# A hybrid decoder layer on one core: attention values with query rows on partitions

## The reference, cut to what matters

```python
sh1, sc1, g1, sh2, sc2, g2 = split(silu(c) @ ada_w + ada_b, 6)
xn = rmsnorm(x, norm1_g) * (1 + sc1) + sh1
q, k, v, ca, cg = split(xn @ w_in)            # x: 1 x 256 x 1024; q, k, v: 8 heads x 64
q, k = rmsnorm(q, q_norm_g), rmsnorm(k, k_norm_g)       # per head
s = q @ k.T * 64**-0.5 + rel_bias[head, t5_bucket(dist)]   # own block of 256: causal
y_attn = softmax(s) @ v
a = causal_dwconv(ca * sigmoid(cg), 31 taps)            # 512 channels
a = silu(group_norm(a, 8 groups))
x = x + g1 * (concat([y_attn, a]) @ w_out)
xn2 = rmsnorm(x, norm2_g) * (1 + sc2) + sh2
u, g = split(causal_dwconv(xn2 @ w_up, 3 taps))         # w_up: 1024 x 5632
x = x + g2 * ((silu(g) * u) @ w_down)                   # w_down: 2816 x 1024
```

## Time and profile before

| | us |
|---|---|
| three runs of the kernel before | 370.85, 366.93, 375.74 |
| median | 370.85 |
| the profiled execution: its time | 369.77 |
| its span in the profile | 368.0 |
| mean granted clock of TensorE in it | 0.981 of full |

### The profile page before, as it was taken

The page is one execution under the profiler, slowest core; times in us unless marked ns, Lnnn a source line. Parts: engine busy times, 40 slices in busy tenths (PEclk is TensorE's granted clock), DMA queues, the critical chain, the costliest instruction groups (busy, mean ns, idle before and its releaser), DMA issues.

```text
span 368.0 us, 6109 instructions
## 1 busy us (share of the span) xinstructions
PE 350.7 (95%) x2401; PEld 297.6 (81%) x2401; DVE 262.7 (71%) x489; ACT 177.6 (48%) x258; POOL 43.3 (12%) x74
## 2 busy tenths in 40 slices
PE   7979899999999998799999999999999999999995
PEld 6658888997553656587999989898989999999984
DVE  2664699979999475548978785857666766768565
ACT  5444733353035648165585655455364553735530
POOL 6281352250000100002300000000000000000000
PEclk9999999999999859899999999999999999999999
DMA  7999987798978750341173555364554545500003
GB/s 283 427 420 421 419 321 287 283 354 346 418 319 339 332 205 24 116 171 57 47 299 130 214 228 216 127 231 135 208 199 156 217 164 188 216 8 1 2 0 114
DMA packets 12797, 79.51 MB, mean 216 GB/s; under 512 B 1368, under 2 KB 2784, under 8 KB 3552
## 3 DMA queue, kind: packets, MB, share of 16 engines
q1 hardware_dynamic: 12560, 78.97, 56.0%
q10 hardware_dynamic: 144, 0.13, 0.1%
q0 software_dynamic: 64, 0.01, 0.0%
HBM read 78.05 MB, written 1.06 MB: 215 GB/s over the span
## 4 chain that ended last, share of the span: by engine, by line
PE 83%; DVE 9%; ACT 3%; issue 2%; DMA 1%; POOL 0%; DVEq 0%; ACTq 0%; POOLq 0%
PE bank L932 25%; PE bank L933 23%; PE bank L934 23%; PE bank L956 3%; PE bank L976 2%; DVE bank L681 1%; PE bank L987 1%; DMA xt<-in_x_t 1%; DVE w_lo L594 1%; PE bank L1199 1%; PE bank L1079 1%; DVE prob L778 1%; PE bank L1001 1%; DVE w_lo L614 1%; PE bank L1132 1%
## 5 line engine op out<-in xcount | busy, mean ns | idle before, releaser
L932 PE MATMUL bank<-act_hi,w_hi 128*128 128x256 f32 x480 | 137.4, 286 | 2.9 <-ACT act_hi L391 1.1
L933 PE MATMUL bank<-act_lo,w_hi 128*128 128x256 f32 x480 | 135.7, 283 | 0.0
L934 PE MATMUL bank<-act_hi,w_lo 128*128 128x256 f32 x480 | 135.7, 283 | 0.0
L594 DVE TENSOR_TENSOR w_lo<-raw,w_hi 128x2048 fp32r<-128x2048 f32 (+1 forms) x44 | 95.2, 2164 | 30.8 <-ACT w_hi L364 30.8
L932 PEld LDWEIGHTS bank<-act_hi,w_hi 128*128 128x128 f32 x480 | 91.8, 191 | 10.7 <-issue 5.3
L364 ACT ACTIVATE w_hi<-raw 128x2048 fp32r<-128x2048 f32 x45 | 85.9, 1908 | 15.2 <-DMA raw<-in_stream 12.4
L933 PEld LDWEIGHTS bank<-act_lo,w_hi 128*128 128x128 f32 x480 | 92.0, 192 | 0.4
L934 PEld LDWEIGHTS bank<-act_hi,w_lo 128*128 128x128 f32 x480 | 91.9, 192 | 0.0
L681 DVE SCALAR_TENSOR_TENSOR bank<-glu,cols,bank 128x256 f32<-128x256 f32 x116 | 46.5, 479 | 0.0
L553 ACT ACTIVATE bias<-bank,cols 128x256 f32<-128x256 f32 x44 | 22.2, 555 | 34.0 <-PE bank L934 34.0
L932 PE MATMUL bank<-w_hi,hid_hi 128*128 128x512 f32 x88 | 34.9, 396 | 0.0
(11 more groups left out here) (172 smaller groups left out, 393.1 us busy)
## 6 DMA issues: line engine op xcount, KB each, us to landing
raw<-in_stream SPq DMA_DIRECT2D x71, 1024.0 KB, 5.1
xt<-in_x_t SPq DMA_DIRECT2D x2, 512.0 KB, 4.6
bias<-toeplitz_rows SPq DMA_DIRECT2D x1, 1024.0 KB, 10.8
xr<-in_x_rows SPq DMA_DIRECT2D x1, 1024.0 KB, 9.8
out<-xmod SPq DMA_DIRECT2D x3, 256.0 KB, 2.0
gates_b<-in_ada_b_gates SPq DMA_DIRECT2D x1, 256.0 KB, 8.5
cols<-in_cols SPq DMA_DIRECT2D x1, 185.0 KB, 5.3
out<-xmod SPq DMA_DIRECT2D x1, 128.0 KB, 1.9
```

What stands on the lines that cost most here:

```text
L594: nc.vector.tensor_tensor(w_lo[:, m % PARTS, cut], slot(*SPLIT[m])[:, cut], w_hi[:, m % PARTS, cut].bitcast(f32), ALU.subtract).then_inc(l ...
L932: nc.tensor.matmul(o, sh, mh, start=first, stop=False)
L933: nc.tensor.matmul(o, sh, ml, start=False, stop=False)
L934: return nc.tensor.matmul(o, sl, mh, start=False, stop=last)
```

## The change

Value matmuls: the transposed probabilities (keys x query rows) become the stationary operand and v (64 columns) the moving one, so that bank 5 gets query rows on partitions and the head's 64 columns beside each other: three matmuls of 64 columns a head. The probabilities are not multiplied by the reciprocals any more; the values are, by DVE out of bank 5 into `att_rows` (scale_rows). For each pair of heads TensorE then transposes att_rows (turn_rows, two transposes) into the upper half of bank 5, where att_hi_part and att_lo_part read. Besides, the lists of the head loop are ordered anew, the modulation rows are turned behind the loop into bank 0, and POOL also subtracts the last 768 columns of "out" 0, 1 and 2.

```diff
-        POOL_LOW = range(3, 10)
+        POOL_LOW = range(3, 13)
+        att_rows = glu_gate[:, :, 0:P]
-        HIGH_AT_HEAD = {0: out 0, 3: out 1, 5: out 2}      LOW_AT_HEAD = {3: out 0, 4: out 1, 7: out 2}
+        HIGH_AT_HEAD = {0: out 0, 1: out 1, 4: out 2, 7: out 3}   LOW_AT_HEAD = {2: out 0, 3: out 1, 5: out 2}
 # POOL
+            for m in POOL_LOW:
+                if m == SP_AT["out", 0]: gn_square(0)
+                elif m == SP_AT["out", 2]: gn_square(1)
+                low_rest(m)
 # ACT
-                act.wait_ge(attended, 2 * j + 2)
-                nc.scalar.activation(act_hi[:, j, :], bank[5][:, 0:SEQ], ACT.Copy).then_inc(att_hi, 1)
+                act.wait_ge(att_turned, j + 1)
+                nc.scalar.activation(act_hi[:, j, :], bank[5][:, SEQ:], ACT.Copy).then_inc(att_hi, 1)
             for h in range(HEADS):
+                turn_copy(h)
                 if h % 2 == 0 and h >= 2: att_hi_part(h // 2 - 1)
                 if h + 1 < HEADS: exps(h + 1)
-                turn_copy(h)
                 if h == 0: gate_out(0)
-                elif h == 2: gate_out(1); mod_rows_out()
-                elif h == 3: gn_deviation()
+                elif h == 3:
+                    gate_out(1); mod_rows_out(); gn_deviation()
+                    nc.scalar.activation(spare[:, 0:1], eps[:, :], ACT.Exp)
                 elif h == 6: gn_swish()
 # DVE
-            def normalise(h): reciprocal; prob *= rtotal (2 instructions); then_inc(normed, 1)
+            def scale_rows(h):
+                dve.wait_ge(exped, 2 * h + 2)
+                nc.vector.reciprocal(rtotal[...], total[...]).then_inc(inverted, 1)
+                dve.wait_ge(inverted, h + 1)
+                dve.wait_ge(attended, h + 1)
+                if h % 2 == 0 and h >= 2: dve.wait_ge(att_turned, h // 2)
+                for t in range(ST):
+                    last = nc.vector.tensor_scalar(att_rows[:, t, 64 * (h % 2):64 * (h % 2) + 64],
+                                                   bank[5][:, 64 * t:64 * t + 64], rtotal[:, 2 * h + t:...], None, ALU.mult)
+                last.then_inc(att_scaled, 1)
             for h in range(HEADS):
-                normalise(h)
-                if 1 <= h < HEADS - 1: add_bias(h + 1)
+                if h >= 1:
+                    scale_rows(h - 1)
+                    if h + 1 < HEADS: add_bias(h + 1)
                 if h % 2 == 0 and h >= 2: att_lo_part(h // 2 - 1)
-                elif h == 3: norm2_columns()
                 elif h == 4:
                     gn_inv
-                elif h == 5:
                     rstd_hi, rstd_lo                         # wait for gn_turned
+                elif h == 5:
                     gn_scale()
-                elif h == 6: mix_parts()
+                elif h == 7: mix_parts()
+            scale_rows(HEADS - 1)
+            split_lo(SP_AT["out", 3])
             att_lo_part(CT - 1)
-            split_lo(SP_AT["out", 3])
+            norm2_columns()
 # TensorE
             def head_turn(h):
-                pe.wait_ge(normed, h + 1)
+                pe.wait_ge(exped, 2 * h + 2)
             def head_values(h):
                 pe.wait_ge(turned_copied, h + 1)
+                if h >= 1: pe.wait_ge(att_scaled, h)
-                matmul(bank[5][r, 0:SEQ], v[:, 0, h * 64:(h + 1) * 64], prob_t[:, h % 2, 0:SEQ])
-                matmul(bank[5][r, P:SEQ], v[:, 1, h * 64:(h + 1) * 64], prob_t[:, h % 2, SEQ:384])
+                matmul(bank[5][:, 0:64], prob_t[:, h % 2, 0:P], v[:, 0, of_head])
+                matmul(bank[5][:, 64:P], prob_t[:, h % 2, P:SEQ], v[:, 0, of_head])
+                matmul(bank[5][:, 64:P], prob_t[:, h % 2, SEQ:384], v[:, 1, of_head])
+            def turn_rows(j):
+                pe.wait_ge(att_scaled, 2 * j + 2)
+                for t in range(ST):
+                    last = nc.tensor.transpose(bank[5][:, SEQ + t * P:SEQ + (t + 1) * P], att_rows[:, t, :], ident[:, :])
+                last.then_inc(att_turned, 1)
                 head_turn(h)
+                if h % 2 == 0 and h >= 2: turn_rows(h // 2 - 1)
+                if h == 2: gn_means(1)                       # before: behind spread_gate(1)
+                elif h == 3: gn_squares()
                 late_ada, spread_gate as before
-                elif h == 3: gn_squares(); turn_mod_rows(4)
                 elif h == 4:
-                    pe.wait_ge(mod_cols_read, 2)
+                    pe.wait_ge(gate_ready, 2); pe.wait_ge(mod_rows_ready, 2)
                     out_part(0, [0, 3])
                     gn_turn()
             out_part(3).then_inc(w_used, 1)
+            turn_rows(CT - 1)
+            pe.wait_ge(biased, 2 * HEADS)
+            turn_mod_rows(0)
             out_part(4)
...
-            pe.wait_ge(biased, 2 * HEADS)
+            pe.wait_ge(mod_cols_read, 2)                     # before the transposes of x2
```

More of the change, by code:

```diff
@@ L190, in hymba_layer @@
         v_ready, rinv_ready, xhat_ready, mixed = sem("v_ready"), sem("rinv_ready"), sem("xhat_ready"), sem("mixed")
-        scores, biased, peaked, exped, inverted, normed, turned, turned_copied, attended, att_hi, att_lo = (
-            sem(s) for s in ("scores", "biased", "peaked", "exped", "inverted", "normed", "turned", "turned_copied",
-                             "attended", "att_hi", "att_lo"))
+        scores, biased, peaked, exped, inverted, turned, turned_copied, attended, att_scaled, att_turned, att_hi, att_lo = (
+            sem(s) for s in ("scores", "biased", "peaked", "exped", "inverted", "turned", "turned_copied", "attended",
+                             "att_scaled", "att_turned", "att_hi", "att_lo"))
         gn_mean, gn_centred, gn_sq, gn_ssq, gn_std, gn_inverted, gn_turned, gn_rs, gn_bc, gn_scaled, gn_silu, mix_hi, mix_lo = (
@@ L326, in _, with low_rest @@
             pool.dma_start(toeplitz_rows, bias_rows[:, :]).then_inc(rows_stored, 16)
-            for m in POOL_LOW:
+            def low_rest(m):
                 pool.wait_ge(hi_done, m + 1)
@@ L333, in _, with gn_square @@
                                         w_hi[:, m % PARTS, POOL_FROM:].bitcast(f32), ALU.subtract).then_inc(lo_rest, 1)
-            for g in range(2):
+            def gn_square(g):
                 pool.wait_ge(gn_centred, g + 1)
@@ L338, in _ @@
                                         conv[:, 2 * g:2 * g + 2, :], ALU.mult).then_inc(gn_sq, 1)
+            for m in POOL_LOW:
+                if m == SP_AT["out", 0]:
+                    gn_square(0)
+                elif m == SP_AT["out", 2]:
+                    gn_square(1)
+                low_rest(m)
             pool.wait_ge(xr_ready, 16)
@@ L509, in _ @@
             att_hi_part(CT - 1)
-            split_hi(SP_AT["out", 3])
             split_hi(SP_AT["up", 0])
@@ L775, in normalise @@
                 dve.wait_ge(inverted, h + 1)
[L776 to L780, removed]
+                dve.wait_ge(attended, h + 1)
+                if h % 2 == 0 and h >= 2:
+                    dve.wait_ge(att_turned, h // 2)
+                for t in range(ST):
+                    last = nc.vector.tensor_scalar(att_rows[:, t, 64 * (h % 2):64 * (h % 2) + 64],
+                                                   bank[5][:, 64 * t:64 * t + 64], rtotal[:, 2 * h + t:2 * h + t + 1],
+                                                   None, ALU.mult)
+                last.then_inc(att_scaled, 1)
             def att_lo_part(j):
                 dve.wait_ge(att_hi, j + 1)
-                nc.vector.tensor_tensor(act_lo[:, j, :], bank[5][:, 0:SEQ], act_hi[:, j, :].bitcast(f32),
+                nc.vector.tensor_tensor(act_lo[:, j, :], bank[5][:, SEQ:], act_hi[:, j, :].bitcast(f32),
                                         ALU.subtract).then_inc(att_lo, 1)
@@ L803, in _ @@
                     gn_centre(1)
-                elif h == 3:
-                    norm2_columns()
                 elif h == 4:
@@ L1205, in head_values @@
                 pe.wait_ge(turned_copied, h + 1)
-                r = slice(64 * (h % 2), 64 * (h % 2) + 64)
+                if h >= 1:
+                    pe.wait_ge(att_scaled, h)
                 if h % 2 == 0 and h >= 2:
                     pe.wait_ge(att_lo, h // 2)
-                nc.tensor.matmul(bank[5][r, 0:SEQ], v[:, 0, h * 64:(h + 1) * 64], prob_t[:, h % 2, 0:SEQ],
-                                 start=True, stop=False)
-                nc.tensor.matmul(bank[5][r, P:SEQ], v[:, 1, h * 64:(h + 1) * 64], prob_t[:, h % 2, SEQ:384],
+                of_head = slice(h * 64, (h + 1) * 64)
+                nc.tensor.matmul(bank[5][:, 0:64], prob_t[:, h % 2, 0:P], v[:, 0, of_head], start=True, stop=True)
+                nc.tensor.matmul(bank[5][:, 64:P], prob_t[:, h % 2, P:SEQ], v[:, 0, of_head], start=True, stop=False)
+                nc.tensor.matmul(bank[5][:, 64:P], prob_t[:, h % 2, SEQ:384], v[:, 1, of_head],
                                  start=False, stop=True).then_inc(attended, 1)
+            def turn_rows(j):
```

(7 more changed lines are left out.)

23 lines of the change are left out of this document (8 added, 15 removed).

## The result

| | median us | runs | ratio to before, 95% interval |
|---|---|---|---|
| before, beside it | 370.2 | 4 | |
| changed kernel | 366.31 | 4 | 0.9882 [0.9834, 0.9930] |
| changed kernel again, in the study | 365.81 | 8 | 0.9896 [0.9854, 0.9938] |
| profiled execution, before / changed | 369.77 / 365.96 | | span 368.0 / 364.2 |

The forecast was 365.5. The ratios leave out executions more than 1.5% above the fastest of the same kernel, the medians hold all of them.

What follows compares the result with a forecast made beforehand. TensorE, busy 95% of the span, bounds the kernel; only its waits, low clock or own work can pay. -9.2 (full clock) + 0.8 (GpSimd) + 3.4 (clock) = -5.0 us, 364.8 from 369.77, stated as 365.5; range 360 to 371.

Steps and rivals of the forecast that it cites:

- the walk: Step-by-step times from the first exponentials through heads 0 to 7 to the output projection's end at 160.0: -9.2 us at full clock.
- Prices of the new operations: Per head or pair: three value matmuls 0.80 us, scale_rows' two PSUM reads 0.18 each, two rows-turn transposes 0.21.
- The hole at head 7: 3.37 us of TensorE idle ahead of head 7's transposes, behind DVE's mix_parts and multiplication; forecast to go.
- The stall at head 6: Rows-turn waits until 137.95 because scale_rows(5) stands behind DVE's split of "out" 2: 1.6 us.
- The stall at head 4 behind ACT's two table loads: Table loads of 1.28 us each delay head 4's copy; TensorE idles 2.1 us behind the first output products.
- The clock's term: One fall between 122 and 130 us, the second gone with its idle: 3.4 us lost, bounds 0 and 8.
- GpSimd's term: POOL's subtractions in the heads may hold DVE's small negative maximum (L768) at heads 2 and 3: +0.8 us.
- a multiplication that leaves the chain of every head: DVE's reciprocal (0.16 us) and multiplication (0.55) no longer stand between exponentials and transposes, which wait for ACT alone.
- full clock throughout: Rival: no low clock, -9.2 us or -8.4 with GpSimd's toll, 361 to 362 us; chance 0.27.
- ACT as the pacer: Rival: ACT's longer list grows the stalls at heads 4 and 6 by 1.5 us each: 369 us; chance 0.19.
- A clock held low by narrow values through all heads: Rival: clock low from near 112 to near 143 us, kernel slower by 5.3 us, 375; chance 0.06.

Runs made afterwards that it cites:

- e8: The changed kernel, unchanged, run again for its spread and a second profile: median 365.81 us, ratio 0.9896.
- e7: The changed kernel with VectorE's split of output tile 2 at head 6 instead of head 5: 363.38 us, ratio 0.9846.
- e10: The changed kernel with e7's edit and five f32 fill matmuls ahead of the transposes of heads 3 and 6: 364.95 us, ratio 0.9859.
- e2: The changed kernel with GpSimd's share of the subtractions undone and its squares behind VectorE's last subtraction again: 364.38 us, ratio 0.9870.
- e6: The changed kernel's lists and GpSimd share, with the values computed as before the change: 368.31 us, ratio 0.9958.
- e9: The kernel before with only the values changed (new matmuls, scaling behind them, rows-turn), on the old lists: 363.56 us, ratio 0.9827.
- e4: The changed kernel with the 16 fill transposes near 12 us replaced by 8 f32 matmuls of 128 columns: 365.96 us, ratio 0.9910.
- e12: The kernel before with the new values and with mix_parts at head 7 instead of head 6, other lists as before: 363.44 us, ratio 0.9828.

## Why the prediction was right, and where not

The second profile (e8) lets the walk be checked, since its loop begins at 105.49, as before. Starts of the values, forecast at full clock against measured: head 0 111.0 / 111.02, head 1 114.8 / 115.01, head 2 120.75 / 120.68. To there the clock was full and the walk is off by 0.2 us at most. Then the clock falls at 122.4, within the 122 to 130 us forecast: head 4 130.25 / 133.05, head 5 134.55 / 137.61, head 6 140.9 / 146.49, head 7 144.75 / 150.23, end 160.0 / 165.21.

- *Prices of the new operations.* Three value matmuls 0.81 us (115.54 to 116.35; forecast 0.80), scale_rows' two instructions 0.47 us together (forecast 0.36), two transposes 0.22 (123.22 to 123.44; forecast 0.21). Right.
- *The hole at head 7.* Closed, and nothing took its place. Right.
- *The stall at head 6.* 1.20 and 1.01 us where 1.6 was forecast, behind VectorE's split, and moving that split behind it (e7) removes it. Right.
- *The stall at head 4 behind ACT's two table loads.* In both profiles of the changed kernel the low clock covered it; in e10, where the clock held from 119 to 134, it shows with 1.46 us ahead of gn_turn (2.1 forecast). Right in kind, too large, and only where the clock is full.
- *The clock's term.* Forecast 3.4 us with one low stretch. In e8 the loop has two: the first lasts 10 us where about 7 were forecast, the second runs from 139.5 to 146.3, beginning just ahead of TensorE's 1.01 us of idle, and the end comes 5.2 us behind the walk. Under-sized: head 4's values are 2.8 us late, and 2.5 more are lost between those of heads 5 and 6. The prediction had no second stretch.
- *GpSimd's term.* +0.8 was forecast. In e8 head 2's values are on time, with L768's successor at most 0.56 us long, and e2 shows no toll. e6 shows where one would have been: on the old multiplication. The step was that the two places where the subtraction and the maximum meet fall on the path; they fell elsewhere, and VectorE's shorter split (1.49 us instead of 2.28) shortened the stall at head 6, which the prediction had priced at nothing. By the Trainium skill (SBUF — State Buffer, Who interferes with whom) the maximum would be held back, and it was (1.37 us against 0.17); the rule held, and the price worked out by it, 2.35 us, was not paid. The other half of that sentence, that a scaling out of PSUM is free of it where the old one was not, came true as well: 0.47 us in the changed kernel, 2.00 and 2.18 instead of 0.55 in e6.
- *What the sum left out* is the spread of executions ahead of the loop, 4.4 us in the first profile.

The two errors have opposite signs, 1.8 us more for the clock and 0.8 less for GpSimd, and their sum, 1.0 us, is what e8's execution is off: 365.81 where 364.8 was worked out. So that the forecast of 365.5 met 366.3 so closely is in part luck. What the prediction did not see is which part pays. It spoke of one hole and of a multiplication that leaves the chain of every head, and priced them in one walk. The runs part them, by their medians: one moved line gives 4.4 of before's microseconds, the layout 6.0, both 6 to 7, the whole change 4. At clock 0.981 it is 4.0, 5.6, 5.4 to 5.6 and 5.4. So the reordered lists, which the walk followed step by step, show no gain on top of the layout: at equal clock the changed kernel and e9 are level (364.3 against 364.1, 363.2 against 362.9), and its runs have the lower clock, 0.972 to 0.985 against 0.979 to 0.986. Why they do is not settled. Low stretches of 3 to 16 us lie at places that recur (20 to 33, 112 to 121, from 122 or 126 on, 140 to 146), and executions differ in which of them they have; e4's profile has the same as e8's.

Of the rivals, full clock throughout is nearest in a single run, 361.93 us at 0.989. ACT as the pacer did not come: it asked for stalls at heads 4 and 6 of 1.5 us more than the walk's 2.1 and 1.6, and they were at most 1.46 (e10) and 1.20 us (the changed kernel). A clock held low by narrow values through all heads did not occur in any profile. e7, e9 and e12, at 363.4 to 363.6, are 6 to 7 us faster than the kernel before; that they also beat the changed kernel holds for the medians alone, since the intervals overlap.

## What to carry to other kernels

Before a redesign takes an operation out of a chain, move the work that stands ahead of that operation on its engine: here one line of the list gave about as much as the whole change by the medians, and half to three quarters of it at equal clock. Try layout and order of the lists apart, since they may close the same hole. Look also at how long the releasing instruction took, and not only at what stood ahead of it: two of e6's three waits for VectorE were waits of VectorE beside GpSimd. Where the time of one kernel spreads with the granted clock, set runs of the same clock beside the medians, and let a second profile tell whether a late start comes in every execution.

## What the runs showed of the hardware

- The clock fell with TensorE busy all the time. In e8 it is busy for 4.00 of 4 us from 118 to 122 at full clock and for 10.00 of 10 from 122 to 132 at 0.52, after values of 64 columns, scores and transposes. The Trainium skill (TensorE: Matmul & The Clock Gate, Part 4, PE-mode transpose) says that a transpose doesn't count as busy the same way; e4, which swapped sixteen of them for matmuls, didn't tell the two apart.
- The mean clock of the kernel before on one chip ran from 0.961 to 0.991 over 25 executions, and its time from 366.9 to 374.7 us. Time does not follow the mean alone: the kernel before took 366.9 us at 0.986 and 368.3 at 0.991.
- A VectorE instruction over two columns, SBUF to SBUF, took 1.37 us instead of 0.17 (138.03 to 139.40) when a GpSimd subtraction of 1.84 us ran beside it (137.53 to 139.37). The two multiplications of e6, SBUF to SBUF, took 2.00 and 2.18 us instead of 0.55 beside one of 1.80 us. The pair of scalings out of PSUM took 0.47 us beside one of 1.80 us (122.16 within 121.16 to 122.96), as without.
